# Differential attention on one core: the keys' low parts as two 64-row multiplications on the two row halves, in place of two 128-row ones against zero-padded queries

## The reference

```python
def diff_attention(q, k, v, ...):
    ...
    def block(qblk):
        s = jnp.einsum('bqhmd,bkhmd->bhmqk', qblk, k, preferred_element_type=f32)
        a = jax.nn.softmax(s, axis=-1)
        w = a[:, :, 0] - lam * a[:, :, 1]
        return jnp.einsum('bhqk,bkhe->bqhe', w.astype(v.dtype), v)
```

## Time and profile before

| | us |
|---|---|
| median of 3 runs | 2687.72 (2687.09 to 2689.8) |
| the profiled execution | 2687.42 |
| its span, first to last instruction | 2685.6 |
| first attention, about | 60 to 325 |
| second attention, about | 1510 to 1761 |

### The profile page before, as it was taken

How to read it: one execution, slowest core, us unless ns; L and a number is a source line. 1 busy time by engine, 2 the same in 40 slices (tenths; PEclk the granted TensorE clock), 3 DMA queues, 4 the chain that set the end, 5 groups by cost and what they waited for, 6 DMA issues and landing times.

```text
span 2685.6 us, 38255 instructions
## 1 busy us (share of the span) xinstructions
PE 2646.9 (99%) x14662; PEld 2139.1 (80%) x14662; DVE 1958.9 (73%) x2311; ACT 1121.8 (42%) x1632; POOL 1367.0 (51%) x898
## 2 busy tenths in 40 slices
PE   8999999999999999999999999999999999999999
PEld 6888877777788888888888766678878888888887
DVE  6777676778767766687778688855876566777775
ACT  6555533342433333344454355532243334444351
POOL 5111100002377777788945322132577777888842
PEclk9999999999999999999999999999999999999999
DMA  4111011113123323454412111112233445544422
GB/s 135 32 44 44 25 47 40 40 33 103 44 83 114 110 79 114 144 174 149 161 48 101 49 40 41 41 39 80 73 103 137 165 141 187 191 156 149 148 65 78
DMA packets 103712, 251.54 MB, mean 94 GB/s; under 512 B 10952, under 2 KB 15024, under 8 KB 100080
## 3 DMA queue, kind: packets, MB, share of 16 engines
q1 hardware_dynamic: 98864, 234.99, 26.9%
q10 hardware_dynamic: 4672, 14.18, 1.4%
HBM read 188.40 MB, written 58.11 MB: 92 GB/s over the span
## 4 chain that ended last, share of the span: by engine, by line
PE 88%; DVE 6%; ACT 2%; POOL 2%; issue 1%; DMA 1%; SPq 0%; DVEq 0%; ACTq 0%; POOLq 0%
PE ps L1254 9%; PE ps L1389 8%; PE ps L1390 8%; PE ps L1256 8%; PE ps L1391 8%; PE ps L1255 8%; PE ps L1439 6%; PE ps L1437 6%; PE ps L1438 6%; PE ps L1612 2%; PE ps L1856 1%; PE ps L1832 1%; PE ps L1842 1%; PE ps L1600 1%; PE ps L1586 1%
## 5 line engine op out<-in xcount | busy, mean ns | idle before, releaser
L1033 POOL TENSOR_TENSOR w_hi<-w_raw,der 128x1024 fp32r<-128x1024 f32 (+1 forms) x52 | 94.0, 1808 | 819.9 <-PE ps L1256 738.9
L1254 PE MATMUL ps<-a_hi,w_hi 128*128 128x512 f32 x1100 | 454.4, 413 | 2.9 <-DVE dq_odd L2003 1.3
L1256 PE MATMUL ps<-a_hi,w_lo 128*128 128x512 f32 x1100 | 430.9, 392 | 0.0
L1255 PE MATMUL ps<-a_lo,w_hi 128*128 128x512 f32 x1100 | 429.5, 390 | 0.0
L1086 POOL TENSOR_TENSOR w_lo<-w_raw,w_hi 128x512 fp32r<-128x512 f32 x212 | 289.2, 1366 | 119.4 <-ACT w_hi L2956 119.3
L2956 ACT ACTIVATE w_hi<-w_raw 128x512 fp32r<-128x512 f32 (+1 forms) x251 | 171.4, 684 | 357.0 <-PE ps L1391 188.2
L2550 DVE TENSOR_TENSOR x<-ps,x 128x512 f32<-128x512 f32 x356 | 236.4, 688 | 31.5 <-PE ps L1439 31.5
L1086 POOL TENSOR_TENSOR w_lo<-asum,w_hi 128x512 fp32r<-128x512 f32 x151 | 209.0, 1384 | 87.4 <-ACT w_hi L2956 87.4
L1254 PEld LDWEIGHTS ps<-a_hi,w_hi 128*128 128x128 f32 x1100 | 207.4, 189 | 49.0 <-issue 8.2
L1256 PEld LDWEIGHTS ps<-a_hi,w_lo 128*128 128x128 f32 x1100 | 206.4, 188 | 45.7
L1255 PEld LDWEIGHTS ps<-a_lo,w_hi 128*128 128x128 f32 x1100 | 207.4, 189 | 33.9
(11 more groups left out here) (496 smaller groups left out, 6743.3 us busy)
## 6 DMA issues: line engine op xcount, KB each, us to landing
fb_wait<-hidden SPq DMA_DIRECT2D x56, 512.0 KB, 3.8
w_raw<-in_w_mix SPq DMA_DIRECT2D x54, 512.0 KB, 3.6
hidden<-hcomb SPq DMA_DIRECT2D x27, 1024.0 KB, 3.9
w_raw<-in_w_f SPq DMA_DIRECT2D x96, 256.0 KB, 3.0
w_raw<-in_w_gu SPq DMA_DIRECT2D x88, 256.0 KB, 2.6
fa_wait<-hidden SPq DMA_DIRECT2D x28, 512.0 KB, 3.9
hidden<-hbuf SPq DMA_DIRECT2D x27, 512.0 KB, 5.6
w_raw<-in_w_ple SPq DMA_DIRECT2D x16, 512.0 KB, 3.5
```

Of the source, the lines that this page charges most:

```text
L1254: mm(ps[:, bank, :], wh, hi[:, k, cols], start=(n == 0), stop=False)
L1255: mm(ps[:, bank, :], wh, lo[:, k, cols], start=False, stop=False)
L1256: last = mm(ps[:, bank, :], wl, hi[:, k, cols], start=False, stop=(n == nk - 1))
```

## The change

The keys' low parts of map `m` are stored anew: those of the first 512 keys in rows 0 to 63, those of the second 512 keys in rows 64 to 127, in one tile of 512 columns for each map (`dkl[n][m]`). The two multiplications of a visit use 64 rows each: keys' half `hf` lies on the rows `64 hf` to `64 hf + 63`. The high queries must then be in both row halves. In the map's own rows they are in `dqs[m]` already; a copy of them in the other rows is `dqc`, one tile for both maps. So there are no zeros any more and no clearing. VectorE writes each map's low keys in two subtractions of 512 columns, and waits for its own end after map 0's. Both multiplications of a visit count `scored`, so the counts of its waits double.

```diff
-        dkl = [at("dkl_even", T, S0 + 4 * KB, F32R), at("dkl_odd", T, 148 * KB, F32R)]
-        dqz = [at("dqz0", T, S0 + 28 * KB, F32R), at("dqz1", T, S0 + 36 * KB, F32R)]
+        dkl = [[at(f"dkl{m}_{n}", HALF, o[m], F32R) for m in range(2)]
+               for n, o in (("even", (S0 + 36 * KB, S0 + 6 * KB)), ("odd", (S0 + 38 * KB, 150 * KB)))]
+        dqc = at("dqc", T, S0 + 28 * KB, F32R)
+
+        def map_rows(m):
+
+            return slice(64 * m, 64 * m + 64), slice(64 * (1 - m), 64 * (1 - m) + 64)
...
             def pad_queries(h):
 
                 sp_.wait_ge(qk_high, 4 * h + 4)
-                sp_.wait_ge(scored, 2 * KT * h)
+                sp_.wait_ge(scored, 4 * KT * h)
                 for m in range(2):
-                    r = slice(64 * m, 64 * m + 64)
-                    sp_.dma_start(dqz[m][r, :].bitcast(F32), dqs[h % 2][m][r, :].bitcast(F32)).then_inc(z_in, 16)
+                    r, o = map_rows(m)
+                    sp_.dma_start(dqc[o, :].bitcast(F32), dqs[h % 2][m][r, :].bitcast(F32)).then_inc(copied_in, 16)
...
             pool.memset(other_q, 0.0).then_inc(cs_clear, 1)
-            for m in range(2):
-                pool.memset(dqz[m][:, :].bitcast(F32), 0.0).then_inc(z_clear, 1)
...
                 for hf in range(2):
-                    last = mm(ps[:, 2 + 2 * m + hf, :], dqz[m][:, t], dkl[h % 2][:, hf * HALF:(hf + 1) * HALF],
-                              start=False, stop=True)
-                last.then_inc(scored, 1)
+                    r = map_rows(hf)[0]
+                    q = dqs[h % 2][m] if hf == m else dqc
+                    last = mm(ps[:, 2 + 2 * m + hf, :], q[r, t], dkl[h % 2][m][r, :], start=False, stop=True)
+                    last.then_inc(scored, 1)
...
-                pe.wait_ge(z_in, 32 * (h + 1))
+                pe.wait_ge(copied_in, 32 * (h + 1))
...
-                dve.wait_ge(scored, 2 * g + m + 1)
+                dve.wait_ge(scored, 4 * g + 2 * m + 2)
...
-                r, o = slice(64 * m, 64 * m + 64), slice(64 * (1 - m), 64 * (1 - m) + 64)
+                r, o = map_rows(m)
                 hi = (dkk if t else dqs)[h % 2][m][r, :].bitcast(F32)
-                ins = tt(dkl[h % 2][r, :] if t else dqs[h % 2][m][o, :], dq[h % 2][r, t, :], hi, ALU.subtract)
+                if t:
+                    for hf in range(2):
+                        c = slice(hf * HALF, (hf + 1) * HALF)
+                        ins = tt(dkl[h % 2][m][map_rows(hf)[0], :], dq[h % 2][r, 1, c], hi[:, c], ALU.subtract)
+                    if m == 0:
+                        step(ins)
+                else:
+                    ins = tt(dqs[h % 2][m][o, :], dq[h % 2][r, 0, :], hi, ALU.subtract)
...
-            act.wait_ge(z_clear, 2)
...
             for m in range(2):
-                r = slice(64 * m, 64 * m + 64)
-                av(dqz[m][r, :], dq[0][r, 0, :], ACT.Copy).then_inc(z_in, 16)
+                r, o = map_rows(m)
+                av(dqc[o, :], dq[0][r, 0, :], ACT.Copy).then_inc(copied_in, 16)
```

More of the change, by code:

```diff
@@ L626, in bass_two_blocks @@
         cs_in = sem("cs_in")
-        z_clear = sem("z_clear")
-        z_in = sem("z_in")
+        copied_in = sem("copied_in")
         swap_dma = sem("swap_dma")
```

## The result

The changed kernel takes 2700.18 us (median of 6 runs, 2697.12 to 2702.78) against 2687.66 us (2687.07 to 2690.83) before: ratio 1.0044, 95% interval 1.0031 to 1.0056, so 12.5 us slower, where 7.3 were forecast and the range ended at 2698.5. Later comparisons gave 1.0040 (1.0026 to 1.0054) and 1.0034 (1.0022 to 1.0047); over all runs the medians are 2698.56 us (17 runs) and 2687.83 us (65 runs), 10.7 us apart. The profiled execution took 2700.54 us, 13.1 more than that of before.

What follows compares the result with a forecast made beforehand. TensorE was taken to bound the kernel, busy 2646.9 of 2685.6 us. Visit terms 4.8 + 2.8 - 0.15 - 0.15 gave +7.3 us on the profiled 2687.42, 2694.7, plus 0.3 for the median: 2695.0; range 2690 to 2698.5.

Steps and rivals of the forecast that it cites:

- Rival 1: First attention's scores: half-height loads are fetched ahead, nothing drains; 2674 us, chance 0.08; with one stop about 2684, 0.04.
- Rival 3: First attention's scores: the pair doesn't run side by side in fp32r; +0.21 us a visit, 2708 us; chance 0.04.
- rival 2: TensorE's waits, mostly behind the first attention, hide more than counted; +3 to +5 us, about 2692; chance 0.07.
- the pair's stream: First attention's scores: two half-height low-part multiplications stream together in 0.21 us, half of plain fp32's 0.42; ceiling 0.23.
- first high part: Start of each score visit on TensorE: the first full-height multiplication of the high parts streams for 0.23 us.
- second with emptying: Next in each score visit: the second full-height multiplication, 0.23 us of streaming and 0.09 of emptying, 0.32 us together.
- half-height load: Before each visit's half-height multiplications: their weight load is not fetched ahead and costs 0.11 us.
- a visit into a projection step: Score visits followed by a projection step: 1.07 us against 0.90 to 0.93, +0.155 us each, 31 counted, 4.8 us.
- into the transposes: Score visits followed by transposes: 1.02 us, next load exposed for 0.06, +0.105 us each, 27 counted, 2.8 us.
- 1.5 us either way for the spread of the runs shown: Whole kernel: allowance for the spread of runs, beside bounds from the terms of 2691.7 to 2696.6 us.
- all behind it as before: Profile after the first attention: that stage grows by 7 us and everything behind it stays as before.
- VectorE at head 0: Subtractions before dq_odd take 0.36 us more, but a short operation's end falls on GpSimd's: 0, bounds 0 and 0.36.

Runs made afterwards that it cites:

- the delay: The kernel before, with the first high part's multiplication done twice in 40 visits (blocks 3 to 7, both maps): 2696.14 us.
- the repeat of before: The kernel before, unaltered, run and profiled once more: 2688.20 us against 2687.37, ratio 1.0003.
- the serial version: The kernel before, with both low-part multiplications on the map's own 64 rows, one after the other: 2710.66 us against 2688.83, ratio 1.0083.
- the two repeats: The changed kernel, unaltered, run and profiled twice more: 2699.55 us, then 2697.10 us.
- VectorE's part alone: The kernel before, with each keys' low part as two subtractions of 64x512 and the wait between the maps: 2688.74 us against 2688.83, ratio 1.0001.
- the second clearings: Second run of the changed kernel with GpSimd's two clearings and ScalarE's wait for them put back: 2698.60 us beside the changed kernel's 2697.10.

## Why the prediction was wrong in size and right in kind

**The mechanism held.** Drain, exposed load, pair, drain, exposed load: all five stand in the rows, the "issue" before a pair's loads was 0.35 us as said, and the first record behind a visit lasts 0.50. Rival 1 (loads fetched ahead) is out by the 64 waits, and doubling the stops doubled the price. Rival 3 (not side by side) was built: it costs 14 us more. Of rival 2 (hidden waits) there is no sign: of 9.27 us of pure streaming in the stage 8.8 reached the median, and what comes back between the stage and 700 us (0.5 in the changed kernel, 0.9 with the delay) comes back in the repeat of before too (0.9), where the stage is no longer.

**The term that failed is the pair's stream, 0.21 us.** From the pair's start to the next load are 0.43 us, less 0.107 of exposed load and 0.09 of emptying 0.233; by the serial version (13.95 us over 61 visits) it is **0.229**. I had halved the two-pass plain fp32 pairs, though the full-height spacing, which I kept as the ceiling, was the same operation in the same format. 60 x 0.02 = 1.2 us: 7.3 + 1.2 = 8.5 against 8.6 measured. By itself this error would have left the result inside the range: 2687.7 + 8.6 is 2696.3. The other terms, forecast and measured: first high part 0.23, 0.23; second with emptying 0.32, 0.32; half-height load 0.11, 0.11; emptying 0.09, 0.09; a visit into a projection step +0.155, +0.175; into the transposes +0.105, +0.12 (the differences are the pair's).

**The step that put the result outside the range** is "1.5 us either way for the spread of the runs shown", together with "all behind it as before". Three runs of before spread over 2.7 us; 65 spread over 4.3 and 17 of the changed kernel over 6.8. In the profiled executions of both kernels two places make most of that: the clock behind the wait for third_lo, and the entry of the feed-forward, where a transfer that lands 1.2 us later costs up to 3.1 us of TensorE. Of five profiled executions without the change two lost 1.3 us or more there (3.0 and 1.4), of nine profiled ones with it, or with a form of it, four (1.4 to 3.1).

That the first comparison came out as high as 2700.18 is in part chance: of the changed kernel's three medians one lies within the range (2697.10), and the one over all runs, 2698.56, at its end.

**VectorE at head 0, "I take 0, bounds 0 and 0.36", left a case out.** What I wrote, that a later start changes nothing if GpSimd's end sets it, is right for an operation that is already caught, as in that profile of before. I left out that a later start can also *get* it caught: in the changed kernel's first profile 0.36 us of work turned into the 1.4 us wait that the late TensorE should no longer have had. It is no fixed price: in the two repeats the operation came ahead of GpSimd's (60.85 and 60.61 us against 61.80 and 60.83), and VectorE's part alone cost nothing that its comparison can tell. On average over profiles, TensorE stands 1.2 us behind before at map 1's first scores in nine executions with the change or a form of it (0.3 to 4.0), and 0.25 in five without (0 to 0.5). Not all of that is VectorE's: 1.8 is the execution above, 4.0 that of the second clearings, and in two (1.3 and 1.7) nothing was caught, but the clock stayed low about twice as long; the other five stand at 0.3 to 0.4.

**What stays open**: the 8.6 us of stage are explained, the other 2.1 of the 10.7 us between the medians are not. The averages just given would make 0.9 of them, but they hang on four executions of nine. Whether the chance places strike the changed kernel more often, or the runs just fell so, these executions don't settle. Nor was it tried why asum's wait for its transfer at the entry is either 2.8 to 3.2 us or 3.9 to 4.1.

## What to carry to other kernels

Half-height pairs save one stream (0.23 us here), and pay 0.39 us whenever full-height work stands on both sides; so count the changes of height, not the multiplications, and gather pairs between two changes until the streams saved exceed the stop, if the waits allow it (two in a row came out about even here; more were not tried). Take a stream's time from the nearest row of the same format, not from half of another's. Where a kernel of before has run only a few times, profile it twice before you call its spread small, and look for the short operations whose start decides between 0.2 and 2 us.

## What the runs showed of the hardware that was not expected

- A change between 128 and 64 rows costs 0.09 us of emptying and 0.107 us of a load that isn't fetched ahead (0.06 us for the load of 128-column transposes), in each direction, and it is paid anew at every change (61 more pairs of them: 24.2 us). The rule of the Trainium skill that speaks of a drain (TensorEngine Tiling (Array Packing), Key Properties) gets its price by that; the load is as much of it again. Between two pairs of 64 rows the loads are fetched ahead as between full-height multiplications.
- A VectorE operation on 128x8 takes 0.17 us, or 1.90 when it starts 0.02 us behind a GpSimd operation of 1.9 us on 128x1024; moved elsewhere, the stall goes along with it (1.42 and 2.19 us). The Trainium skill (SBUF — State Buffer, SBUF: two separate sides) says that GpSimd's operations share a pair of ports with VectorE's in a two-port mode or with two inputs from SBUF, and that whichever starts first holds it to its end; the trace agrees, as the stalled operation ends with GpSimd's (62.82 and 62.79 us). Whether that operation, which has one input, runs in such a mode no run here shows. VectorE's evictions of 128x512 out of PSUM were not held: the two of dq_odd took 1.29 us from 61.02 us in the changed kernel's second repeat, while GpSimd's operation ran from 60.83 to 62.75.
- Behind the same wait of 2.1 to 3.0 us TensorE's clock stayed at 2.4 GHz in some executions (a granted clock of 1.00 from 36 to 42 us) and fell to 1.2 GHz for some microseconds in others (0.53 to 0.79). The kernel before did both (1.00 and 0.72). The fall cost 1.4 to 1.6 us, and 2.6 and 2.8 in the two executions that show the lowest figures (0.59 and 0.53).
